# Four sums of weight quarters of a feed-forward projection: made by accumulating transfers that GpSimd issues, instead of by VectorE

## What is computed

```python
x = x + rms_norm(merged @ w_o[l], norm_mix_post[l])
h2 = rms_norm(x, norm_ffn_pre[l])
gu = h2 @ w_ffn_in[l]                              # 512 x 2048 times 2048 x 11264
f = (silu(gu[..., :D_FF]) * gu[..., D_FF:]) @ w_ffn_out[l]
x = x + rms_norm(f, norm_ffn_post[l])
```

## Time and profile before

| what | value |
|---|---|
| median of the runs | 2452.33 us |
| span of the profiled execution | 2450.2 us |
| its clock for TensorE | full in all 40 slices but for rounding |
| TensorE busy | 2430.8 us of the span |
| VectorE busy | 2127.4 us |
| ScalarE busy | 1174.6 us |
| GpSimd busy | 118.5 us |

### The profile page before, as it was taken

How to read it: one execution, slowest core, us unless ns; L and a number is a source line. 1 busy time by engine, 2 the same in 40 slices (tenths; PEclk the granted TensorE clock), 3 DMA queues, 4 the chain that set the end, 5 groups by cost and what they waited for, 6 DMA issues and landing times.

```text
span 2450.2 us, 45714 instructions
## 1 busy us (share of the span) xinstructions
PE 2430.8 (99%) x19390; PEld 1897.1 (77%) x19390; DVE 2127.4 (87%) x2296; ACT 1174.6 (48%) x1408; POOL 118.5 (5%) x93
## 2 busy tenths in 40 slices
PE   9999999999999999999999999999999999999998
PEld 4444445888888888858648888888888888888887
DVE  7998788788888888798898999999999998777776
ACT  5235334444444444456564555555555554444443
POOL 1000020000000000012310000000000000000011
PEclk9999999999999999999999999999999999999999
DMA  6221223233323323343343333333333346433436
GB/s 260 103 104 69 96 79 104 100 119 114 117 104 116 120 99 122 116 168 138 106 145 112 128 126 132 130 125 131 131 126 129 132 156 252 142 119 121 132 117 250
DMA packets 97208, 317.91 MB, mean 130 GB/s; under 512 B 9504, under 2 KB 26272, under 8 KB 95648
## 3 DMA queue, kind: packets, MB, share of 16 engines
q1 hardware_dynamic: 97056, 315.81, 37.4%
...
## 4 chain that ended last, share of the span: by engine, by line
PE 82%; DVE 13%; issue 3%; ACT 1%; DMA 1%; POOL 0%; DVEq 0%; SPq 0%; ACTq 0%; POOLq 0%
PE psum L1985 16%; PE psum L1987 16%; PE psum L1986 16%; PE psum L1978 5%; PE psum L1979 5%; PE psum L1980 5%; PE psum L2323 5%; PE psum L2324 5%; PE psum L2325 5%; DVE region_f L1359 3%; DVE wq L1119 2%; ACT wq L631 1%; DVE region_f L1678 1%; DVE region_t L1126 1%; DVE stage L1142 0%
## 5 line engine op out<-in xcount | busy, mean ns | idle before, releaser
L1119 DVE SCALAR_TENSOR_TENSOR wq<-stage,wq 128x1024 f16<-128x1024 f32 (+1 forms) x758 | 902.4, 1200 | 232.2 <-ACT wq L631 227.5
L631 ACT ACTIVATE wq<-stage 128x1024 f16<-128x1024 f32 (+1 forms) x758 | 776.6, 1030 | 678.3 <-DVE stage L1142 276.9
L1987 PE MATMUL psum<-region_t,wq 128*128 128x256 f16 x2368 | 645.5, 273 | 0.0
L1986 PE MATMUL psum<-region_t,wq 128*128 128x256 f16 x2368 | 645.5, 273 | 0.0
L1985 PE MATMUL psum<-region_t,wq 128*128 128x256 f16 x2368 | 645.5, 273 | 0.0
L1985 PE MATMUL psum<-region_f,wq 128*128 128x256 f16 x1776 | 484.1, 273 | 1.7 <-DVE work L1157 1.5
L1987 PE MATMUL psum<-region_f,wq 128*128 128x256 f16 x1776 | 484.1, 273 | 0.0
L1986 PE MATMUL psum<-region_f,wq 128*128 128x256 f16 x1776 | 484.1, 273 | 0.0
L1978 PE MATMUL psum<-region_f,wq 128*128 128x512 f16 x720 | 273.4, 380 | 1.2 <-DVE wq L1119 1.2
L1980 PE MATMUL psum<-region_f,wq 128*128 128x512 f16 x720 | 273.2, 379 | 0.0
L1979 PE MATMUL psum<-region_f,wq 128*128 128x512 f16 x720 | 273.2, 379 | 0.0
...
## 6 DMA issues: line engine op xcount, KB each, us to landing
stage<-w_ffn_in_chunks SPq DMA_DIRECT2D x176, 512.0 KB, 3.9
stage<-w_gate_chunks SPq DMA_DIRECT2D x128, 512.0 KB, 3.8
...
stage<-w_in_chunks SPq DMA_DIRECT2D x52, 512.0 KB, 5.6
stage<-w_o_chunks SPq DMA_DIRECT2D x32, 512.0 KB, 4.3
stage<-w_ffn_out_chunks SPq DMA_DIRECT2D x32, 512.0 KB, 3.9
stage<-w_branch_chunks SPq DMA_DIRECT2D x24, 512.0 KB, 3.4
t_spill<-region_f SPq DMA_DIRECT2D x22, 512.0 KB, 3.2
```

The lines of the kernel that those rows point to most:

```text
L631: nc.scalar.activation(dst, stage[:, SLOT[q], 0:UNIT_W[u]], ACT.Copy, scale=WSCALE).then_inc(hi_ready, 1)
L1119: V.scalar_tensor_tensor(out=slot[:, 1, 0:w], in0=stage[:, SLOT[q], 0:w], scalar=WSCALE, in1=slot[:, 0, 0:w], op0=ALU.mult, op1=ALU.subtra ...
L1986: mm(to, w[:, 0, w_at:w_at + P], x[:, 1, :], start=False, stop=False, skip_group_check=True)
L1987: return mm(to, w[:, 1, w_at:w_at + P], x[:, 0, :], start=False, stop=stop, skip_group_check=True)
```

## The change

For the 40 Strassen chunks of the feed-forward input, and only there:

- The quarters are loaded in another order (`ADDED_ORDER`), and each of the four sums is made by a DMA that GpSimd issues: it reads a quarter again from memory and adds it to the slot of `stage` (`accum_op=ALU.add`). The slot of unit u + 1 holds quarter 2 plus 3; then quarter 0 is added to it for u + 3, and quarter 1 for u + 6; the slot of u gets quarter 2 for u + 4.
- The signs are turned so that all are additions: `sum_halves_signed` for the activations, and the factor of `f_product` is negative for these chunks (a third column of `fscale`).
- The products stand in another order (`strassen_added`), and `hi` of units u + 1, u + 3, u + 4, u + 6 waits for the DMAs' semaphores. `keep_product(u + 2)` becomes `keep_product(u + 3)` and comes behind `hi(u + 6)`.
- VectorE no longer runs `make_s1` to `make_s4` in the loop; those of the output projection stay.
- SyncE's waits at the loop's end move by one unit.

```diff
+def added_units(width=UW):
+    u, q = len(UNIT_AT), len(FREED)
+    UNIT_AT.extend((q + 1, q + 3, q, q + 3, q + 1, q + 2, q + 3))
+    UNIT_SUMS.extend((0,) * SU)
+    UNIT_W.extend((width,) * SU)
+    FREED.extend((u + 3, u + 5, u + 6, u + 7))
...
-            sp.wait_ge(unit_done, DONE[last + 1])
+            sp.wait_ge(unit_done, DONE[last + 2])
             bring_sums(0, 3)
-            sp.wait_ge(unit_done, DONE[last + 2])
+            sp.wait_ge(unit_done, DONE[last + 3])
             bring_sums(0, 1)
             spill_sums(FP - 2)
-            sp.wait_ge(unit_done, DONE[last + 3])
...
+            def add_quarter(c, u, i, done):
+                q = UNIT_AT[u]
+                nc.gpsimd.dma_start(stage[:, SLOT[q], :], w_ffn_in[4 * c + i], accum_op=ALU.add).then_inc(done, 16)
+
+            def sum_cd(c):
+                u = U_FS + SU * (c - PLAIN_FFN) + 1
+                q = UNIT_AT[u]
+                pool.wait_ge(landed[SLOT[q]], LANDS[q])
+                add_quarter(c, u, 0, cd_added)
+
+            def add_quarters():
+                sum_cd(PLAIN_FFN)
+                for c in range(PLAIN_FFN, FT):
+                    u = U_FS + SU * (c - PLAIN_FFN)
+                    pool.wait_ge(lo_ready, u + 1)
+                    add_quarter(c, u + 4, 3, quarters_added)
+                    pool.wait_ge(lo_ready, u + 2)
+                    add_quarter(c, u + 3, 1, quarters_added)
+                    pool.wait_ge(lo_ready, u + 4)
+                    add_quarter(c, u + 6, 2, quarters_added)
+                    if c + 1 < FT:
+                        sum_cd(c + 1)
...
+                elif U_FS <= u < U_X and i == 1:
+                    act.wait_ge(cd_added, 16 * (c + 1))
+                elif U_FS <= u < U_X and i in (3, 4, 6):
+                    act.wait_ge(quarters_added, 48 * c + (48 if i == 6 else 32))
...
                 hi(u + 5)
-                keep_product(u + 2, cs, 0)
                 hi(u + 6)
+                keep_product(u + 3, cs, 0)
...
-            make_s3(U_FS, CS_F)
             lo(u + 8)
             lo(u + 9)
-            make_s2(U_FS, CS_F)
-            make_s1(U_FS, CS_F)
...
                 lo(u + 4)
                 lo(u + 5)
-                make_s4(u, cs)
...
                 lo(u + 6)
-                make_s3(*following)
+                if c + 1 == FT:
+                    make_s3(U_X, CS_F)
...
                 lo(u + 8)
-                make_s2(*following)
-                make_s1(*following)
+                if c + 1 == FT:
+                    make_s2(U_X, CS_F)
+                    make_s1(U_X, CS_F)
...
+            def strassen_added(s, u, cs, units, chunks, turn):
+
+                pe.wait_ge(lo_ready, at(u + 1, units, turn))
+                pe.wait_ge(copied, at(3 * cs, 3 * chunks, turn))
+                product(u, Q1, lambda i: s[:, 1, 0, i], True)
+                pe.wait_ge(lo_ready, at(u + 2, units, turn))
+                pe.wait_ge(c_read, at(3 * cs, 3 * chunks, turn))
+                product(u + 1, Q3, lambda i: tset[:, 2, i], True)
+                pe.wait_ge(lo_ready, at(u + 3, units, turn))
+                product(u + 2, Q2, lambda i: tset[:, 3, i], True)
+                pe.wait_ge(lo_ready, at(u + 4, units, turn))
+                pe.wait_ge(copied, at(3 * cs + 1, 3 * chunks, turn))
+                product(u + 3, Q1, lambda i: tset[:, 1, i], False)
+                pe.wait_ge(lo_ready, at(u + 5, units, turn))
+                pe.wait_ge(copied, at(3 * cs + 2, 3 * chunks, turn))
+                product(u + 4, Q1, lambda i: tset[:, 0, i], False)
+                pe.wait_ge(lo_ready, at(u + 6, units, turn))
+                product(u + 5, Q4, lambda i: s[:, 1, 1, i], True)
+                pe.wait_ge(lo_ready, at(u + 7, units, turn))
+                pe.wait_ge(c_read, at(3 * cs + 1, 3 * chunks, turn))
+                product(u + 6, Q3, lambda i: s[:, 0, 1, i], False)
```

More of the change, by code:

```diff
@@ L136 @@
 for c in range(FT - PLAIN_FFN):
-    strassen_units(CS_F + c)
+    added_units()
 assert len(UNIT_AT) == U_X and len(FREED) == Q_X
 for n in range(NX - 1):
-    strassen_units(CS_X + n, PIECES[n % 3] * P)
-strassen_units(CS_X + NX - 1, PIECES[-1] * P, (0, 1, 2, 4, 5, 3, 6))
+    strassen_units(CS_F + n, PIECES[n % 3] * P)
+strassen_units(CS_F + NX - 1, PIECES[-1] * P, (0, 1, 2, 4, 5, 3, 6))
 assert len(UNIT_AT) == U_END
@@ L220, in block_program @@
         irms = sb("irms", [P, 4, NB], F32)
-        fscale = sb("fscale", [P, 2], F32)
+        fscale = sb("fscale", [P, 3], F32)
         mean2 = sb("mean2", [P, NB], F32)
@@ L332, in block_program @@
         hi_ready, lo_ready, sums_made, unit_done = sem("hi_ready"), sem("lo_ready"), sem("sums_made"), sem("unit_done")
+        cd_added, quarters_added = sem("cd_added"), sem("quarters_added")
         copied, c_read, sig_ready, sig_used = sem("copied"), sem("c_read"), sem("sig_ready"), sem("sig_used")
@@ L591, in _ @@
                         pool.wait_ge(x2sq_used, b + 1)
+                    add_quarters()
                 if phase == 0:
@@ L618, in hi @@
                 q = UNIT_AT[u]
+                c, i = (u - U_FS) // SU, (u - U_FS) % SU
                 if UNIT_SUMS[u]:
                     act.wait_ge(sums_made, UNIT_SUMS[u])
+                elif U_FS <= u < U_X and i == 1:
+                    act.wait_ge(cd_added, 16 * (c + 1))
+                elif U_FS <= u < U_X and i in (3, 4, 6):
+                    act.wait_ge(quarters_added, 48 * c + (48 if i == 6 else 32))
                 else:
@@ L1163, in c12_c11, with sum_halves_signed @@
                                 copies[:, 0:2, :], ALU.add).then_inc(c_read, 1)
+            def sum_halves_signed(t):
+                V.tensor_tensor(t[:, 2, :], t[:, 2, :], t[:, 0, :], ALU.subtract).then_inc(dve_step, 1)
+                dve.wait_ge(dve_step, step.up())
+                V.tensor_tensor(t[:, 0, :], t[:, 1, :], t[:, 0, :], ALU.subtract).then_inc(dve_step, 1)
+                dve.wait_ge(dve_step, step.up())
+                V.scalar_tensor_tensor(out=t[:, 1, :], in0=t[:, 2, :], scalar=-1.0, in1=t[:, 1, :],
+                                       op0=ALU.mult, op1=ALU.subtract).then_inc(dve_step, 1)
+                dve.wait_ge(dve_step, step.up())
+                V.scalar_tensor_tensor(out=t[:, 3, :], in0=t[:, 1, :], scalar=-1.0, in1=t[:, 3, :],
+                                       op0=ALU.mult, op1=ALU.subtract).then_inc(t_made, 1)
             def sum_halves(t):
@@ L1722, in f_product @@
                 V.scalar_tensor_tensor(out=f_pair[c // 2 % 2][:, at_:at_ + 2, :], in0=up.rearrange("p (h s) -> p h s", h=2),
-                                       scalar=fscale[:, 1:2], in1=cb[:, 0, :].rearrange("p (h s) -> p h s", h=2),
+                                       scalar=fscale[:, 1:2] if c < PLAIN_FFN else fscale[:, 2:3], in1=cb[:, 0, :].rearrange("p (h s) -> p h s", h=2),
                                        op0=ALU.mult, op1=ALU.mult).then_inc(f_ready, 1)
@@ L1756, in x_sums @@
                 dve.wait_ge(v_made, 2 * i + 2)
-                sum_halves(t_ffn[:, i % 2])
+                sum_halves_signed(t_ffn[:, i % 2])
             def x_low(i):
@@ L1780, in _ @@
             V.tensor_scalar(fscale[:, 1:2], fscale[:, 0:1], S * UNSCALE, None, ALU.mult).then_inc(fscale_ready, 1)
+            V.tensor_scalar(fscale[:, 2:3], fscale[:, 0:1], -S * UNSCALE, None, ALU.mult).then_inc(fscale_ready, 1)
             V.tensor_scalar(mean2[:, :], rms[:, 2, :], fscale[:, 0:1], None, ALU.mult).then_inc(dve_step, 1)
@@ L1785, in _ @@
             dve.wait_ge(rinv_copied, 1)
-            dve.wait_ge(fscale_ready, 1)
+            dve.wait_ge(fscale_ready, 2)
             evict_ffn(0)
@@ L1876, in x_piece @@
             def x_piece(n):
-                u, cs = U_X + SU * n, CS_X + n
+                u, cs = U_X + SU * n, CS_F + n
                 following = (u + SU, cs + 1) if n + 1 < NX else None
@@ L1906, in last_piece @@
             def last_piece():
-                c, u, cs, b = PAIRS - 1, U_END - SU, CS_X + NX - 1, 4 * ((PAIRS - 1) % 2)
+                c, u, cs, b = PAIRS - 1, U_END - SU, CS_F + NX - 1, 4 * ((PAIRS - 1) % 2)
                 lo(u + 4)
@@ L2313, in _ @@
                 for c in range(4):
-                    strassen(h2, U_FS + SU * c, CS_F + c, False, 4 * SU, 4, turn)
+                    strassen_added(h2, U_FS + SU * c, CS_F + c, 4 * SU, 4, turn)
             def half_product(u, bank, half, n, x, first, last):
@@ L2433 @@
 STRASSEN_ORDER = [0, 2, 3, 1]
+ADDED_ORDER = [3, 0, 1, 2]
 def kernel(**inputs):
@@ L2460 @@
     w_ffn_in = _halves(up)
-    w_ffn_in[PLAIN_FFN:] = w_ffn_in[PLAIN_FFN:, STRASSEN_ORDER]
+    w_ffn_in[PLAIN_FFN:] = w_ffn_in[PLAIN_FFN:, ADDED_ORDER]
     w_ffn_in[:2] = _by_k(up[:, :4 * P])
```

1 line of the change is left out of this document (removed).

## The result

The changed kernel takes 2669.45 us (median of 2 runs, 2664.63 and 2674.28); before it is 2452.33 us. The ratio is 1.0887, with a 95% interval of 1.0839 to 1.0934: slower by 217 us.

A forecast was written before the change was run, and what follows sets the result against it. TensorE's matmul stream was taken to bound the kernel before; the chain's 9.2 + 14.4 = 23.6 us per chunk, 5.3 us more, times 40 gave 211 us, so 2663 us, range 2476 to 2880 us.

The forecast's parts named there:

- The likeliest case: Chain through the added DMAs sets the loop: chunks of 19.6 to 28.2 us, 2501 to 2847 us, chance 0.72.
- the ring: Closed dependency from the end of one chunk's product u + 4 to the next's: 9.2 us + L3 + L6.
- L3: Time from release to landing of the add for u + 3, put at 7.8 us.
- L6: Time from release to landing of the add for u + 6, put at 6.6 us.
- Removed sums worth nothing: Four VectorE sums per chunk, 4.9 us, taken out of the loop: worth 0 on the path.
- The keep between neighbours, 0.63 us: Products u + 3 and u + 4 on Q1 with the copy between: 0.63 us per chunk, 25 us over 40.
- The chain: Adds of a chunk in sequence with ScalarE and VectorE: 23.6 us per chunk, 5.3 us more than 18.3.
- The first term: From the end of product u + 4 through keep, hi(u + 1) and its lo: 2.6 us.
- L3 + L6 = 14.4 us: Landing times of the adds for u + 3 and u + 6 together; below 9.8 us they would cost nothing.
- Double price of an add: Each DMA add reads memory and its destination, so it costs the transfer engines double: four take 10.7 to 12.5 us.
- Rival 1, adds hidden: Adds land within about 5 us of release, only the keep costs in the loop: 2477 us, chance 0.15.
- Rival 2, the engines as the bound: Transfer engines bound the loop, adds at four loads' price: 32 us per chunk, 3000 us; chance 0.12.

The follow-up runs named there:

- e4: Kernel before, with VectorE's sums, but the two products on Q1 made neighbours and the keep behind hi(u + 6); 2487.22 us.
- e9: e7 with the next chunk's add for u + 1 issued right behind the add for u + 4; 2613.85 us.
- e12: e9 with VectorE's low part of f moved behind lo(u + 8), the next chunk's lo(u + 1); 2585.26 us.
- e1: Changed kernel with keep_product(u + 3) moved ahead of hi(u + 6); 2693.11 us.
- e3: Changed kernel with 13 unread matmuls of 512 columns on TensorE ahead of its wait for the keep before product u + 4; 2668.76 us.
- e10: Changed kernel with GpSimd issuing the add for u + 3 ahead of the add for u + 4; 2654.31 us.
- e11: e10 with the 13 matmuls of e3 ahead of the wait for the keep; 2604.71 us.
- e2: Changed kernel with plain copies from GpSimd in place of the adds, so the sums are left out; 2491.08 us.
- e5: e1 without the add for u + 4, its sum left out; 2603.85 us.
- e6: e1 without the add for u + 1, its sum left out; 2675.46 us.
- e7: e1 with all four adds, the one for u + 3 issued ahead of the one for u + 4; 2598.19 us.

## Why the prediction was right, and where its steps were not

The time was forecast as 2663 us and is 2669 us. A chunk was forecast as 23.6 us and is 23.65. The likeliest case came, with the wait at the forecast place and for the forecast reason. That the total came out so closely is luck: four terms of the ring were off by 0.6 to 1.7 us and cancelled out. One turn from the trace, and the mean of 38 turns:

| term | predicted us | this turn us | mean us |
|---|---|---|---|
| keep, hi, lo up to the release of the add for u + 3 | 2.6 | 3.5 | 3.4 |
| L3 | 7.8 | 6.1 | 6.5 |
| hi(u + 3), lo(u + 3) | 2.3 | 2.3 | 2.3 |
| L6 | 6.6 | 6.0 | 6.0 |
| hi(u + 6), keep, start of product u + 4 | 1.5 | 1.4 | 1.4 |
| product u + 4 | 2.8 | 4.5 | 4.1 |
| sum | 23.6 | 23.8 | 23.7 |

- *Removed sums worth nothing.* Right: VectorE's busy time fell from 17.3 to 12.9 us per chunk (12.4 us were forecast), and no time came back, since TensorE had no wait there to lose.
- *The keep between neighbours, 0.63 us.* The size holds for the copy alone (0.64 in e4). By e4's time it is 0.89 us per chunk, as the keep also stands behind hi(u + 6).
- *The chain.* Its order is in the trace step by step. The first term left out that lo(u + 1) stands behind VectorE's joins and low part of f, 1.0 us here and more where another wait doesn't cover it (e9, e12).
- *L3 + L6 = 14.4 us* was too large: 12.1 us in this turn, 12.5 us in the mean. The base of 5.8 us from the row of a 1024 KB load was nearly the median landing itself (5.8 us), so most of the crowding I added on top was not there. That the queue ahead of the add for u + 3 matters was right in kind, but in the changed kernel the two issues lie 4.4 us apart in the mean and not 2.6 us, so that little is left to wait for. Its own turns show it: where they are under 4 us apart (10 turns) the add for u + 3 lands after 7.5 us, else (24 turns) after 5.8 us. In e1 and e3, with some 3.3 us between them in almost every turn, it is 8.4 and 7.5 us in the mean.
- *The clock.* Not in the sum at all: product u + 4 takes 4.5 us in this turn instead of 2.8 us, most of it at a granted clock of 0.51 that follows 3.6 us of idling. By e10 and e11 it costs 50 us when the add for u + 3 is first in the queue. It is not a share of the 217 us that could be had by itself: in the changed kernel taking it away gained nothing (e3).
- *Double price of an add.* 2.0 against the same copies. Right.
- *Rival 1, adds hidden.* It did not come, but e2 shows it: with landings of 4.1 us the time is 2491 us, 14 us above the 2477 us given for it (and 40 us above the kernel before, outside its noise, though under the 2% that the prediction took for no change). The Trainium skill, DMA: Bandwidth & Descriptors, section "Anatomy of one DMA — SWDGE (gpsimd) path", gives 2.0 us plus bytes at 436 GB/s, an estimate of 3.2 us for 512 KB and 4.4 us for twice the bytes; GpSimd's plain copies took 4.1 us in the median and 3.6 at best, the adds 5.8 and 5.3, so the measurement decides against it here.
- *Rival 2, the engines as the bound.* Not as a total (0.79 busy; e5 against e6). But in bursts they are full, and this makes landing times depend on the order of issue.

The traces also allow the ring to be added up for every experiment. Means of 34 turns in us: from the start of keep(u + 4) to GpSimd's issue of the add for u + 3; from there to hi(u + 3); to the issue for u + 6; to hi(u + 6); to the next keep(u + 4). L3 and L6 count from the issue here, 0.3 us later than in the table above.

| kernel | keep to issue | L3 | hi, lo | L6 | hi(u + 6) to keep | turn |
|---|---|---|---|---|---|---|
| changed | 3.7 | 6.2 | 2.6 | 5.7 | 5.5 | 23.7 |
| e1 | 5.1 | 8.4 | 2.6 | 5.7 | 2.8 | 24.6 |
| e3 | 3.8 | 7.5 | 2.6 | 5.6 | 4.2 | 23.7 |
| e5 | 5.1 | 5.9 | 2.6 | 5.6 | 2.8 | 22.0 |
| e6 | 4.4 | 8.5 | 2.6 | 5.7 | 2.8 | 24.0 |
| e7 | 4.5 | 6.4 | 2.6 | 5.6 | 2.8 | 21.9 |
| e9 | 4.5 | 6.3 | 2.6 | 6.1 | 2.8 | 22.3 |
| e12 | 3.5 | 5.5 | 2.6 | 7.3 | 2.8 | 21.7 |
| e10 | 3.8 | 5.7 | 2.6 | 5.9 | 5.6 | 23.5 |
| e11 | 3.8 | 5.7 | 2.6 | 6.0 | 4.2 | 22.2 |

In e1 the last part is 2.7 us shorter, but the first is 1.4 us and L3 2.2 us longer; in e3 the last part is 1.2 us shorter and L3 1.3 us longer. e9 is 16 us slower than e7: its add for u + 6 comes 0.5 us later, now that the one for u + 1 stands ahead of it, and the first part stays as it was. In e12 the first part is 1.0 us shorter and L3 0.8 us, but L6 1.1 us longer. How a landing time follows from what else is under way is not resolved further; SyncE's loads in particular were never taken away.
